# Rounded x rows made and stored in the first batch, first state-space head on the common timetable

## What is computed

```
h    = rmsnorm(x) * gain                 # 1024 x 2048
proj = h @ w_in                          # columns: 6 HGRN2 heads (A), 5 band attention (B), 5 retention (C)
ya   = per head: S_t = diag(f_t) S_{t-1} + k_t i_t^T ; o_t = S_t^T silu(q_t)   (chunked, 64 frames)
yb   = per head: softmax attention over the own chunk and the 8 before it, with a bias table
yc   = per head: retention with rotary q and k, in chunks
y    = concat(ya, yb, yc) * silu(gates)
out  = rmsnorm(x + y @ w_out)
```

## Time and profile before

| | |
|---|---|
| median of the runs | 1774.76 us |
| profiled execution | 1771.45 us |
| its span | 1769.6 us |
| PE busy | 1713.2 us (97%) |
| mean granted TensorE clock | 0.993 |
| DMA traffic | 416.47 MB, 235 GB/s |

### The profile page before, as it was taken

The page is one execution under the profiler, slowest core; times in us unless marked ns, Lnnn a source line. Parts: engine busy times, 40 slices in busy tenths (PEclk is TensorE's granted clock), DMA queues, the critical chain, the costliest instruction groups (busy, mean ns, idle before and its releaser), DMA issues. The chain is left out here.

```text
span 1769.6 us, 28246 instructions
## 1 busy us (share of the span) xinstructions
PE 1713.2 (97%) x10536; PEld 1414.9 (80%) x10536; DVE 1169.8 (66%) x1722; ACT 673.3 (38%) x1038; POOL 837.4 (47%) x602
## 2 busy tenths in 40 slices
PE   7999999999999999999999889999999999999996
PEld 6888888888888888888787668887888877888885
DVE  7756675454656555656569776787665448778886
ACT  4333334332422455444552523332334233333342
POOL 4544454544444766656534344444434330355552
PEclk9999999999999999999999899999999999999998
DMA  8999798896998766776777922333333269777876
GB/s 263 334 318 346 253 318 284 287 311 230 339 337 312 245 237 233 258 241 228 247 265 250 312 94 89 109 97 97 97 111 122 79 204 348 247 252 253 285 251 231
DMA packets 216012, 416.47 MB, mean 235 GB/s; under 512 B 24506, under 2 KB 25279, under 8 KB 215876
## 3 DMA queue, kind: packets, MB, share of 16 engines
q1 hardware_dynamic: 200746, 367.51, 61.5%
q10 hardware_dynamic: 15130, 47.15, 7.6%
HBM read 339.05 MB, written 75.51 MB: 234 GB/s over the span
## 5 line engine op out<-in xcount | busy, mean ns | idle before, releaser
L890 POOL TENSOR_TENSOR w_sum<-in_raw,in_raw 128x512 f32<-128x512 f32 x219 | 302.0, 1380 | 290.1 <-PE prj L952 153.1
L952 PE MATMUL prj<-in_hi,w_hi 128*128 128x512 f32 x840 | 328.8, 391 | 9.4 <-DVE w_lo L2247 8.4
L952 PE MATMUL prj<-in_hi,w_lo 128*128 128x512 f32 x840 | 327.6, 390 | 0.0
L952 PE MATMUL prj<-in_lo,w_hi 128*128 128x512 f32 x840 | 327.6, 390 | 0.0
L914 POOL TENSOR_SCALAR w_hi<-w_sum 128x512 fp32r<-128x512 f32 x63 | 102.8, 1631 | 262.3 <-DMA w_sum<-in_w 245.2
L1378 ACT ACTIVATE w_hi<-w_sum 128x512 fp32r<-128x512 f32 x219 | 135.3, 626 | 165.2 <-POOL w_sum L890 161.3
L952 PEld LDWEIGHTS prj<-in_hi,w_hi 128*128 128x128 f32 x840 | 158.0, 188 | 44.2 <-issue 9.4
L907 POOL TENSOR_TENSOR w_lo<-in_raw,w_hi 128x512 fp32r<-128x512 f32 x88 | 120.5, 1374 | 150.0 <-ACT w_hi L1378 150.0
L923 POOL TENSOR_TENSOR raws<-raws 128x512 f32<-128x512 f32 x80 | 111.3, 1394 | 164.4 <-DMA raws<-in_wo 164.2
L952 PEld LDWEIGHTS prj<-in_lo,w_hi 128*128 128x128 f32 x840 | 158.1, 188 | 33.2 <-issue 0.5
L952 PEld LDWEIGHTS prj<-in_hi,w_lo 128*128 128x128 f32 x840 | 158.1, 188 | 32.7
(11 more groups left out here) (187 smaller groups left out, 3021.1 us busy)
## 6 DMA issues: line engine op xcount, KB each, us to landing
in_raw<-in_wi SPq DMA_DIRECT2D x528, 256.0 KB, 4.4
raws<-in_wo SPq DMA_DIRECT2D x184, 256.0 KB, 3.8
arena<-z_scratch ACTq DMA_DIRECT2D x56, 512.0 KB, 4.6
z_scratch<-acc_in SPq DMA_DIRECT2D x88, 256.0 KB, 4.9
y_in<-y_scratch SPq DMA_DIRECT2D x80, 256.0 KB, 4.7
mv_hi<-comb_scratch SPq DMA_DIRECT2D x72, 256.0 KB, 4.6
mv_lo<-comb_scratch SPq DMA_DIRECT2D x72, 256.0 KB, 5.2
w_sum<-in_w SPq DMA_DIRECT2D x60, 256.0 KB, 2.9
```

Of the source, the lines that this page charges most:

```text
L890: nc.gpsimd.tensor_tensor(w_sum[wslot(n)][:], in_raw_buf(a), in_raw_buf(b), ALU.add if sign > 0 else ALU.subtract).then_inc(in_wsum, 1)
L952: last = nc.tensor.matmul(out, wt[wslot(n)][:, i % GRAN, :], mv[j % 2][:, i, :], start=(i == 0 and wt is w_hi and mv is in_hi), stop=(i == ...
```

## The change

All four quarters of x get their rounded parts in the first batch. Sets 0 and 1 are two of them already; the other two are the first pieces of sets 5 and 6, which are loaded anyway. For idx 32 to 47 ACT now also rounds the loaded piece itself (`pure_high`) into the other half of its buffer, DVE takes the rest (`pure_low`) over the first half, and ACT's own DMA queue stores both (`store_pure`, two transfers of 256 KB), one step later. The operands of sets 5 and 6 move from steps 4 to 11 of their product to its steps 2, 3, 5, 6, 8, 9, 11 and 12. Their loads stand in SP's order 2 steps later for idx 32 and 33, 3 for idx 34 to 39, 4 for idx 40 to 47, and wait until the stores out of their buffer have landed. `comb_scratch` gets a layout in which the two halves of a row can be loaded by one transfer, so `load_x` has two transfers of 512 KB in the place of three of 256 KB, and `h_high`, `h_low` and `H_DUE` go. Head 0 of A takes the slots of the others.

```
-LEVEL_AT_SLOW = [8, 9, 11, 12, 14, 15, 17]
...
-    comb_dram = nc.dram_tensor("comb_scratch", (7, HK, 2, P, HALF), F32, kind="Internal").ap()
+    comb_dram = nc.dram_tensor("comb_scratch", (2, HK, P, 9, HALF), F32, kind="Internal").ap()
...
             j, p = divmod(v, IN_PAIRS)
+            if j in (4, 5):
+                return [HK * j + PURE_AT.index(p)] if p in PURE_AT else []
+        PURE0 = 4 * HK
+        PURE_AT = [2, 3, 5, 6, 8, 9, 11, 12]
...
-            return ((LEVEL_AT, 16, 18, 20, 22, 23) if u > 0 else
-                    (LEVEL_AT_SLOW, 18, 20, 22, 24, 25))
+            return LEVEL_AT, 16, 18, 20, 22, 23
...
                 if idx >= 2:
                     sp.wait_ge(in_comb_lo, HK + idx - 1)
+                if idx - 2 >= PURE0:
+                    sp.wait_ge(xe_in[e], entry_free(e, idx // 2))
...
-                j = k // HK
+                parts = slice(1, 9, 7) if k < HK else slice(0, 3, 2)
                 for n, mv in enumerate((mv_hi, mv_lo)):
-                    sp.dma_start(mv[:, k, half(j)].bitcast(F32), comb_dram[j, k % HK, n]).then_inc(x_row_sem(k), 16)
-                sp.dma_start(x_row(k)[:, half(1 - j)], xT[k][:, half(1 - j)]).then_inc(x_row_sem(k), 16)
+                    sp.dma_start(mv[:, k, :].bitcast(F32).rearrange("p (s t) -> p s t", s=2),
+                                 comb_dram[n, k % HK, :, parts, :]).then_inc(x_row_sem(k), 16)
...
-                    at_step = max(v + 2, OPEN)
+                    at_step = max(v + (2 if idx < PURE0 + 2 else 3 if idx < PURE0 + HK else 4), OPEN)
...
+            def pure_high(idx):
+                e, k = idx % 2, HK * in_terms(idx)[0][0] + idx % HK
+                nc.scalar.activation(entry_r[e][:, half(1)], x_entry[e][:, half(0)], ACT.Copy,
+                                     scale=gain_sb[:, k:k + 1]).then_inc(pure_hi, 1)
+            def store_pure(idx):
+                e, at = idx % 2, 8 if idx < PURE0 + HK else 0
+                act.wait_ge(pure_lo, idx - PURE0 + 1)
+                for n, part in enumerate((1, 0)):
+                    act.dma_start(comb_dram[n, idx % HK, :, at, :], entry_r[e][:, half(part)].bitcast(F32)).then_inc(xe_in[e], 16)
...
             for v in range(IN_STEPS):
                 for idx in in_comb_at(v):
                     in_comb_start(idx)
+                for idx in in_comb_at(v - 1):
+                    if idx >= PURE0:
+                        store_pure(idx)
                 if 2 <= v < IN_STEPS:
                     in_w_high(2 * v + 4)
                     in_w_high(2 * v + 5)
                 for idx in in_comb_at(v):
                     in_comb_high(idx)
+                    if idx >= PURE0:
+                        pure_high(idx)
...
+            def pure_low(idx):
+                e, k = idx % 2, HK * in_terms(idx)[0][0] + idx % HK
+                dve.wait_ge(pure_hi, idx - PURE0 + 1)
+                stt(out=entry_r[e][:, half(0)], in0=x_entry[e][:, half(0)], scalar=gain_sb[:, k:k + 1],
+                    in1=entry_r[e][:, half(1)].bitcast(F32), op0=ALU.mult, op1=ALU.subtract).then_inc(pure_lo, 1)
```

More of the change, by code:

```diff
@@ L239, in build @@
         sq_first = over("sq_first", [P, HK, HALF], arena_at + 12 * row)
+        rstd_at = next_at()
         rstd = sb("rstd", [P, SEQ])
@@ L250, in build @@
         x_entry = [x_even, rstd]
+        entry_r = [over("x_even_r", [P, SEQ], part_at, F32R), over("rstd_r", [P, SEQ], rstd_at, F32R)]
         in_raws = [over(f"in_raw{m}", [P, HALF], (at + 15 * row, at + 31 * row, stage_at)[m // 2] + m % 2 * row // 2)
@@ L390, in build @@
         drained = [sem("mix0_drained"), sem("mix1_drained")]
-        h_hi = sem("h_hi")
+        pure_hi = sem("pure_hi")
         ones_ready = sem("ones_ready")
-        h_lo = sem("h_lo")
+        pure_lo = sem("pure_lo")
         ss_ready = sem("ss_ready")
@@ L507, in in_comb_at, with entry_stores, entry_free @@
             j, p = divmod(v, IN_PAIRS)
+            if j in (4, 5):
+                return [HK * j + PURE_AT.index(p)] if p in PURE_AT else []
             return [HK * j + p - OPEN] if j < 6 and OPEN <= p < OPEN + HK else []
-        entry_loads = [[len(in_terms(idx)) for idx in range(e, IN_COMBS, 2)] + [1] * HK for e in range(2)]
+        PURE0 = 4 * HK
+        PURE_AT = [2, 3, 5, 6, 8, 9, 11, 12]
+        ENTRY_USES = IN_COMBS // 2
+        entry_loads = [[len(in_terms(idx)) for idx in range(e, IN_COMBS, 2)] for e in range(2)]
+        def entry_stores(e, uses):
+            return 2 * len([idx for idx in range(e, 2 * uses, 2) if idx >= PURE0])
+        def entry_free(e, uses):
+            return 16 * (sum(entry_loads[e][0:uses]) + entry_stores(e, uses))
         def entry_count(e, use):
-            return 16 * sum(entry_loads[e][0:use + 1])
+            return 16 * (sum(entry_loads[e][0:use + 1]) + entry_stores(e, use))
         SQUARED = [0, 2, 3]
@@ L768, in _ @@
                     sp.dma_start(relrow, relb).then_inc(const_in, 16)
+                if st == ALL_STEPS - 4:
+                    for e in range(2):
+                        sp.wait_ge(xe_in[e], entry_free(e, ENTRY_USES))
                 if ALL_STEPS - 4 <= st < ALL_STEPS - 2:
@@ L985, in project @@
                     if g == STD0:
-                        pe.wait_ge(h_lo, at + 1)
+                        pe.wait_ge(x_row_sem(k), X_ROW_FREE + 32)
                     for wt, mv in ((w_hi, mv_hi), (w_hi, mv_lo), (w_lo, mv_hi)):
@@ L1440, in load_z @@
                 act.dma_start(arr(dst), z_dram[t]).then_inc(arrived, 16)
-            due = {"hi": IN_GRANULES + 4, "row": 0, "tile": STD0, "step": IN_STEPS}
+            due = {"hi": IN_GRANULES + 4, "tile": STD0, "step": IN_STEPS}
             def in_first(st):
@@ L1460, in until @@
                     due["hi"] += 1
-                while due["row"] < KB and H_DUE[due["row"]] <= slot:
-                    h_high(due["row"])
-                    due["row"] += 1
                 while due["tile"] < DIRECT and MID_SLOTS + 2 * NG * (due["tile"] - STD0 + 1) <= slot:
@@ L1540, in _ @@
             act.wait_ge(comb_out[0], 256 * 4)
+            act.wait_ge(xe_in[0], entry_free(0, ENTRY_USES))
             load_z(b_tile(0) + 2, VT, z2_in)
@@ L2156, in a_query @@
                 silu_finish(a_silu(u), Q, A_DK ** -0.5, Q)
-            due = {"step": IN_STEPS + 2 * MID_PAIRS, "row": 0}
+            due = {"step": IN_STEPS + 2 * MID_PAIRS}
             def until(slot):
@@ L2164, in until @@
                     due["step"] += 1
-                while due["row"] < KB and H_DUE[due["row"]] <= slot:
-                    h_low(due["row"])
-                    due["row"] += 1
             def a_unit(u):
@@ L2268, in _ @@
                     in_comb_low(idx)
+                    if idx >= PURE0:
+                        pure_low(idx)
                 if v == 6 * IN_PAIRS + 4:
@@ L2278, in _ @@
                     dve.wait_ge(rstd_ready, 2)
+                    dve.wait_ge(xe_in[1], entry_free(1, ENTRY_USES))
                     nc.vector.tensor_copy(rstd[:], mix[1][:]).then_inc(rstd_ready, 1)
```

7 lines of the change are left out of this document (2 added, 5 removed).

## The result

The changed kernel takes 1824.45 us (median of 4 runs, 1821.15 to 1828.2), the kernel before in the same comparison 1774.32 (4 runs, 1771.96 to 1776.66). The ratio is 1.0283, 95% interval 1.0259 to 1.0307: 50 us slower (46 to 54), where the prediction had 32 and a range from 1785 to 1826. The profiled execution of after took 1828.2 us, its span 1826.4. That is the longest of its four, while the profile of before is a short one, so the two profiles differ by 56.8 us and the medians by 50.1.

A forecast was written before the change was run, and what follows sets the result against it. PE, busy 1713 of 1770 us, was taken to bound the kernel. Passage -11, product 4 +5.2, product 5 +36.6 and low clock +1 made +31.8 us: 1806.6 us against the median 1774.76, range 1785 to 1826.

The forecast's parts named there:

- The chain in product 5: SP's queue, idx 40 to 47: each next load waits behind the previous operand's store; PE loses 36.6 us (20.6 to 48.6).
- L: Time from SP's first issue of an operand's two x transfers to ACT's start on them: 5 us, bounds 3 to 6.5.
- 8L - 3.4: Product 5's total PE wait from the chained loads, as a formula in L: 36.6 us, bounds 20.6 and 48.6.
- Rival 3: L grows to 6.3 behind raw weights and tile stores; product 5 costs 47, product 4 costs 9: 1821 us, chance 0.15.
- the low clock behind the last wait: End of product 5: some microseconds of PE at 1.2 GHz, costing 1 us, bounds 0 to 3.
- The Trainium skill's fit: About 2 us fixed plus bytes at 436 GB/s per transfer: L 3.2, product 5 costing 22; not used in the sum.
- Rival 2: SP's queue does not serialise; each product 5 load is late only for itself, 4.4 us: 1773.4 us, chance 0.05.
- Two signs of the prediction: PE's product 5 waits: released by POOL's L907 or ACT's L1378, the larger ones behind idx 41, 43, 45, 47.
- Product 4: Idx 34 to 38, loaded later: three PE waits of L - 3.8, with extras 5.2 us (bounds 1.6 and 9.7).
- The 0.8 for the second of each pair: Product 4: ACT issues store_pure ahead of the weights, costing each second operand 0.8 us, 2 x 0.8 in the sum.
- The passage: Move to the single tiles: DVE waits go, row transfers bind, row 11's load at about 985; gain 11 us, bounds 0 to 22.
- Rival 4: The passage gains only 0 to 5 us because its rows are DMA bound: +38 to +43, about 1815 us, chance 0.12.

The follow-up runs named there:

- experiment 1: Changed kernel with the x loads of idx 34 to 47 back at their old distance, 2 steps, in SP's order: 1769.93 us, ratio 0.9988.
- experiment 2: Changed kernel with the loads of idx 40 to 47 at 3 steps in place of 4 in SP's order: 1789.51 us, ratio 1.01.
- experiment 3: Kernel before with only the new operand steps and load places in SP's order, no added rounding or stores, old rows and timetable: 1821.39 us, ratio 1.0284.
- experiment 4: Changed kernel with the stores of set 6 (idx 40 to 47) two steps later in SP's order, v + 6 for v + 4: 1824.17 us, ratio 1.0296.
- experiment 5: Changed kernel with only the loads of idx 34 to 39 late (v + 3), those of idx 40 to 47 back at v + 2: 1781.21 us, ratio 1.0058.
- 6, product 5: Changed kernel with only the loads of idx 40 to 47 late (v + 4), those of idx 34 to 39 back at v + 2: 1813.58 us, ratio 1.0237.
- experiment 9: Kernel of experiment 1 with PE taking row 15 before row 14 in the first single tile: 1769.92 us, ratio 0.9983.
- experiment 8: Kernel of experiment 1 with head 0 of A back on its late timetable: 1769.09 us, ratio 0.9981.

## Why the prediction was right, and where its sizes were off

By the medians the sum of -11 + 5.2 + 36.6 + 1 should have been -2.2 + 11.3 + 43.7 = 52.8, beside the 50.1 (46 to 54) between the two kernels. The mechanism and its place held, and every term was too hopeful, by 6 to 9 us.

The -2.2 is the whole of experiment 1 and so contains its small loss in product 4. The traces separate the stages. The table gives the us that each kernel loses against the kernel before in a stage (a minus is a gain), counted by PE's matmuls (24 a step in the first batch) and by ACT's eviction of the second single tile. The numbers of the rows are those of the experiments. Each row is one execution, and the column before step 60 shows how much chance it holds.

| kernel | before step 60 | product 4 | product 5 | from there to the second single tile |
|---|---|---|---|---|
| after | 2.9 | 12.6 | 45.0 | -3.9 |
| 1, loads back | 0.3 | 1.6 | 0.0 | -5.1 |
| 2, one step later | 1.6 | 11.0 | 7.3 | -1.8 |
| 3, order alone | 0.0 | 12.1 | 37.1 | 0.6 |
| 4, stores later | 2.2 | 12.3 | 42.9 | -3.8 |
| 5, product 4 | 0.4 | 11.2 | 0.0 | -1.9 |
| 6, product 5 | 0.2 | 2.5 | 42.6 | -1.6 |
| 9, row 15 first | 0.0 | 1.9 | 0.1 | -5.5 |

**The chain in product 5 (36.6 + 1, measured 43.7 by the medians, 42.6 and 45.0 in the traces).** It ran as written. SP stood in the store's wait behind every load; from ACT's start on the first of a pair to SP's issue of the next load it took 5.87, 5.86, 7.47 and 5.86 us (forecast 6.05), from the second to the next pair's first 10.59, 10.65 and 10.72 (10.3). L was 6.06, 5.34, 5.48, 4.82, 5.62, 5.03, 6.27 and 5.21, mean 5.48 where I took 5: 8L - 3.4 is then 40.4, 3.8 more, and the step of 7.47 and the 0.3 of the longer ones bring it to 42. I had drawn L from a mix of pairs and single transfers; a pair, which is what stands in the chain, lies nearer to the 6.0 and 4.8 of the earlier trace rows, and the sixteen pairs of these two products in before landed in 3.8 to 6.5 us, mean 5.7. Rival 3's L of 6.3 did not come. The added stores have no share in L: without them (experiment 3) the mean is 5.52. Whether raw weights and tile stores ahead of a load lengthen it, as that rival had it, no run separates. The rest of the term, 2 to 3 us, is the low clock behind the last wait, in my 0 to 3.

The Trainium skill's fit ("DMA: Bandwidth & Descriptors", "Anatomy of one DMA"), which I had weighed and set aside, would as an estimate have made product 5 cost 22. The Trainium skill gives that fit for transfers issued by GpSimd, and these are SP's; the measured L of 5.48 and the 43.7 us decide against it for this use.

Rival 2, that SP doesn't serialise, is refuted by the idle SP. That the store is what holds it was only half of it: experiment 4 shows a second holder of nearly the same length, which the prediction named as queued behind the wait but not as a wait of its own. Two signs of the prediction came otherwise: the profile names no releaser for the waits where it was to be POOL or ACT, and the wait behind idx 47 (4.07 us) is no larger than the one before it (4.12).

**Product 4 (5.2, measured 11.3 by the medians and 11.2 to 12.6 in the traces, above the bound of 9.7).** The waits have the form forecast: L of the three firsts, 6.27, 5.87 and 5.63, less 3.8 makes 2.5, 2.1 and 1.8, and PE waited 2.67, 2.28 and 2.09. That is 7.0 us, where L = 5 gave 3.6. The 0.8 for the second of each pair did not appear beside them. What was missing is the clock. I wrote that within a chain it costs nothing, which is right for product 5 and was silently carried over to product 4, where there is no chain: PE there is the pace-setter again right behind each wait. In after the stretches 380 to 388, 404 to 412 and 420 to 428 us were granted 0.79, 0.79 and 0.80, about 3 x 8 x 0.2 = 5 us lost beside 7.0 idle, 12 in all. The 11.3 is counted over experiment 1 and leaves out the 1.6 us that product 4 loses there. The row that would have told it was before me: 0.79 around a wait of 3.24, which I used at the passage only. (I read PE's idle share in the three windows of the earlier trace rows around the passage as a fifth; it is a quarter. No term rests on it.)

**The passage (gain 11, measured 2 to 5).** By the last column of the table the passage gained 3.9 us in after, 1.6 to 5.5 in the other kernels that have the new rows and the early timetable. Rival 4, with a gain of 0 to 5, had this term; its total of 1815 was too low, because the other two terms were short as well. What goes, went: no wait for the low part of a row is left, and the transposes are held for 0.15 us. What comes is the transfers, as forecast, but sooner and for longer. PE's waits in experiment 1, where nothing earlier disturbs the passage:

```profile
1009.20 1.22 PE L1002 MATMUL prj<-mv_hi,w_hi 128*128 128x512 f32 x2 [4.43 <-DMA mv_lo<-comb_scratch]
...
1024.00 0.73 PE L1002 MATMUL prj<-mv_hi,w_hi 128*128 128x512 f32 x2 [3.22 <-DMA mv_lo<-comb_scratch]
```

and SP's queue there, with its tile's eviction on ACT:

```profile
987.60 0.81 SPq L692 DMA_DIRECT2D z_scratch<-acc_in  x2
988.45 1.14 SPq L681 DMA_DIRECT2D mv_hi<-comb_scratch  x1
...
1001.51 3.72 SPq L681 DMA_DIRECT2D mv_hi<-comb_scratch  x1
1005.27 3.21 SPq L681 DMA_DIRECT2D mv_lo<-comb_scratch  x1
```

```profile
1027.05 1.02 ACT L1486 ACTIVATE stage<-prj 128x1024 f32<-128x1024 f32 x1 [25.47 <-PE prj L1002]
```

Row 11's load goes at 988.45 and not at 985: SP still waits for an accumulation there, 2.4 us earlier than before and not 6. From there 35 us at 385 GB/s lead to 1023.5, and the last rows were let go at 1024.0, so the bytes and the rate were right. But I let the tile end with the last landing; a row's matmuls and a weight granule still follow, 3 us, to 1027.05. That is 4.2 us under the 1031.24 before, though this kernel came out of the first batch 1.9 us behind; by the next tile's eviction 3.2 us of the lead are left, so the passage gave 5 to 6 us here, the most but one of the traces. The medians have 2.2 us for the whole kernel. The nine last rows carry 2.4 MB more than in the old form, 6 us at 385 GB/s; no run took those bytes away, so that share is worked out and not shown.

## What to carry to other kernels

When a load is moved down an in-order queue, look for the first instruction behind it that waits for what is made of that load, and for every other wait in that queue that the consumer's engine feeds: each closes a loop, one turn of it per operand, and the time per turn is what to compare with PE's work per operand. Here one line, which delays loads by one step and by two, turned a change worth 2 to 3 us into a loss of 50. A short wait of a pace-setting TensorE is to be priced with its clock (in experiment 5, 7.3 us idle and 11.2 us of time), and work moved off one engine is worth only what the next limit, here the bytes, leaves of it.

## What was not expected of the hardware

- Whether the clock falls with a short wait is not fixed by its length. In products 4 and 5 of the six kernels with late loads (after and experiments 2 to 6) PE has 19 waits of 2.0 to 3.0 us. With 11 of them some microseconds were granted at the level of 1.2 GHz, with 8 the clock stayed at 1.00: in after it fell with 2.67, 2.28 and 2.09 us and stayed with 2.80 and 2.55; in experiment 2 it stayed with 2.11 and 2.10. With all 22 waits of 3.1 us and more it fell.
- The landing of a pair of 256 KB loads shows no dependence on traffic: the mean of the eight pairs of a product is 5.8 and 5.5 us in before at 291 and 284 GB/s, 5.8 and 5.2 in experiment 1 at 320 and 316, 5.4 and 5.5 in after at 290 and 210, and 5.1 and 5.5 in experiment 3 at 259 and 187. Single pairs took 3.8 to 7.6 us.
- The issue of a 512 KB transfer of a row on SP took 0.4 to 1.5 us as a rule; 3.72 and 3.21 us once in experiment 1 at 391 GB/s, 3.98 and 2.90 in experiment 9, 2.56 and 4.52 in after. Full DMA engines are not the whole reason: in experiment 8 they moved 393 to 401 GB/s in the same stretch and no issue took over 1.73. The cause stays open.
